# The first expert layer of a two-block transformer kernel: half tiles of 64 rows, two experts at a time in the two column halves of TensorE, in plain fp32

## The chip, the cores and the metric

The kernel runs on one core of a Trainium2 chip. A core has TensorE (matrix products, results in PSUM), VectorE, ScalarE and GpSimd, and SyncE, whose queue issues most of the DMA transfers. The metric is the device time of one execution in microseconds; lower is better.

## The reference, cut to what matters

The whole program is two transformer blocks of two layers each, on 256 tokens of width 1024 (the first block also carries 256 context tokens). The change concerns the mixture of experts of the first layer. It sees 512 tokens, latent and context together:

```python
scores = sigmoid(t @ router_w)
# best group of 4 experts by the sum of its two best scores + bias, then the two best experts in it
combine = one_hot(expert_idx, 16) * normalised_scores          # two experts for each token
def expert(wg, wu, wd, gate_col):                              # wg, wu [1024, 512], wd [512, 1024]
    return gate_col[:, None] * ((silu(t @ wg) * (t @ wu)) @ wd)
out = sum of expert(...) over the 16 experts
```

All arrays are fp32. An expert's three matrices are 2.1 MB each, 6.29 MB together.

## The kernel before, in words

The program is a row of stages with a barrier behind each. The method `experts(layer, tokens)` is the stage of an expert layer: layer 0 with 512 tokens, layer 1 with 256.

The stage begins with the routing. TensorE computes the logits and turns the tokens to rows, which SyncE stores in a DRAM buffer `h_tok`; VectorE ranks the scores and works out, for every token and each of its two experts, a slot: expert e's first 128 tokens have the slots of tile e, and tokens beyond 128 go to overflow tiles 16, 17 and so on. There are `NTILE = 16 + 7 = 23` tiles for 512 tokens, a number fixed at build time, since nothing is known of the routing then. All 23 are computed; an overflow tile that no token needs computes with old weights, because its DMA has a condition (`cond=`, a register loaded from `overflow_in_use_int`) and is skipped.

For each tile GpSimd gathers the token rows from `h_tok` (`tile_rows`), TensorE turns them (`turn_x`, eight transposes) and multiplies: gate (G) and up (U), four pieces each, then down (D), four pieces, of which each is a weight buffer of 128 x 1024 and 512 KB. TensorE runs G and U of tile i, then D of tile i - 1 (`segment(i)`), with `turn_x(i + 1)` ahead of D and `turn_hidden(i)`, four transposes, behind it. The weights lie in the ring areas A (gate), B (up), C and D (down), one expert at a time; a piece is refilled with the next tile's as soon as it is read. The order of the transfers is the order in which SyncE's queue is written: gather results and other stages' panels (`ring.load`, line 83) stand in the same queue.

The products are split in three: ScalarE copies each weight piece to a rounded type (`w_hi`), VectorE forms the remainder (`w_lo`), the same for the turned rows and for the hidden state, and `product` sums hi x hi, hi x lo and lo x hi. ScalarE and VectorE run five pieces ahead (`LEAD`), in six slots.

Results of a tile are copied from PSUM to `tile_out` and stored in `y_slots`. At the end GpSimd waits for all stores, gathers each token's two rows back, and they are mixed, turned and added to the residual.

Of the kernel before, what the change touches and what calls it, by code (L numbers as in the profile page):

```python
# [9 lines left out]
U32 = mybir.dt.uint32  # L10
ALU = mybir.AluOpType
ACT = mybir.ActivationFunctionType
AX = mybir.AxisListType

P = 128
D = 1024
KD = D // P
SEQ = 256
TT = 2 * SEQ
# [12 lines left out]
for _name, _w in VECTORS:  # L32
# [6 lines left out]
CONSTS = [("ident", P), ("ones", P), ("upper", P), ("lower", P), ("up64", P), ("lo64", P),  # L39
          ("xup64", P), ("xlo64", P), ("upper_x", P), ("lower_x", P), ("tie", 16), ("half", 2), ("ropef", 2), ("pair_sum", 2),  # L40
          ("swap_mla", P), ("swap_nsa", P), ("rot_rows", 1), ("causal_add", 2 * P), ("cmp_mask", 32), ("cmp_add", 32)]
ROUTING = [("route_row", P), ("route_base", 16), ("route_over", 16), ("route_before", 256), ("tile_first", 24), ("token_id", 4)]
RCOL, _n = {}, 0
for _name, _w in ROUTING:
    RCOL[_name] = _n
# [1 line left out]
NROUTE = _n  # L47
# [44 lines left out]
@contextmanager  # L92
def stage(nc, names):

    handles = {name: nc.alloc_semaphore(name=f"{name}_{nc.next_id()}") for name in names.split()}
    with nc.Block() as block:  # L96
        yield block, handles
    nc.clear_and_free_semaphores(list(handles.values()))
    nc.all_engine_barrier()


def chain(eng, sem, base=0):

    n = [0]

    def link(ins):
        n[0] += 1
        ins.then_inc(sem, 1)
        eng.wait_ge(sem, base + n[0])
        return n[0]  # L110
    return link


class Program:
# [1025 lines left out]
    def experts(self, layer, tokens):  # L1140
# [4 lines left out]
        nt = tokens // P  # L1145
# [25 lines left out]
        with ExitStack() as ctx:  # L1171
# [54 lines left out]
            with stage(nc, names) as (block, s):  # L1226
# [49 lines left out]
                @block.gpsimd  # L1276
                def _(pool):
                    pool.wait_ge(s["who_done"], 1)
                    pool.wait_ge(s["h_stored"], 16 * nt)
                    for i in range(NTILE):  # L1280
                        if i >= 2:
                            pool.wait_ge(s["x_turned"], i - 1)
                        nc.gpsimd.indirect_dma_start(
                            out=xt[:, i % 2, :], out_offset=None, in_=self.h_tok,
                            in_offset=bass.IndirectOffsetOnAxis(ap=who[:, i:i + 1], axis=0),
                            bounds_check=tokens - 1, oob_is_err=False).then_inc(s[f"xt_in{i % 2}"], 16)
                    pool.wait_ge(s["x_turned"], NTILE)
                    pool.wait_ge(s["stored0"], 16 * ((NTILE + 1) // 2))
                    pool.wait_ge(s["stored1"], 16 * (NTILE // 2))
                    pool.wait_ge(s["rows_done"], 1)  # L1290
                    for t in range(nt):
                        if t >= 2:
                            pool.wait_ge(s["back_turned"], t - 1)
                        for w, (into, sem) in enumerate(((xt, "y0_in"), (y, "y1_in"))):
                            nc.gpsimd.indirect_dma_start(
                                out=into[:, t % 2, :], out_offset=None, in_=self.y_slots,
                                in_offset=bass.IndirectOffsetOnAxis(ap=both_i[:, t, w:w + 1], axis=0),
                                bounds_check=NTILE * P - 1, oob_is_err=False).then_inc(s[f"{sem}{t % 2}"], 16)

# [173 lines left out]
                def _(dve):  # L1473
# [17 lines left out]
                    def hidden_lo(i):  # L1491
                        dve.wait_ge(s["hh_done"], i + 1)
                        V.tensor_tensor(hl[:].rearrange("p k t -> p (k t)"), ps[:, HB, :],
                                        hh[:].rearrange("p k t -> p (k t)").bitcast(F32), ALU.subtract).then_inc(s["hl_done"], 1)
# [92 lines left out]
                    for i in range(NTILE + 1):  # L1587
                        for q, n in enumerate(segment(i)):
                            if n + LEAD < NPIECE:
                                lo(n + LEAD)  # L1590
                            if i < NTILE:
                                if q == 0 and i >= 1:
                                    hidden_lo(i - 1)
                                if q == 7:
                                    hidden(i)
                                if q == (9 if i else 7) and i + 1 < NTILE:
                                    x_lo(i + 1)
                        if i == NTILE - 1:
                            hidden_lo(i)

                    def add(t):
                        dve.wait_ge(s["back_turned"], t + 1)
# [1398 lines left out]
def routing_constants():  # L3001
    c = np.zeros((P, NROUTE), np.float32)
    i, e = np.arange(P), np.arange(16)
    for name, a in (("route_row", i), ("route_base", P * e), ("route_over", P * (15 - e)),
                    ("route_before", (e[None, :] < e[:, None]).reshape(-1)), ("tile_first", P * np.arange(24))):
        c[:, RCOL[name]:RCOL[name] + len(a)] = a
    c[:, RCOL["token_id"]:RCOL["token_id"] + 4] = i[:, None] + P * np.arange(4)[None, :]
    return c
# [86 lines left out]
def everything(p, stop=None):  # L3095
# [4 lines left out]
    if stop == "mix0":  # L3100
        return p.dump()
    p.rms_norm(x, h, KD, TT, lambda k, c: p.scale_mod[:, 1, k, c:c + 1], lambda k, c: p.m(0, 3, k, c))
    p.experts(0, TT)
    if stop == "moe0":
        return p.dump()
    p.rms_norm(x, h, KD, TT, lambda k, c: p.scale_mod[:, 2, k, c:c + 1], lambda k, c: p.m(1, 0, k, c), permuted=True)
# [38 lines left out]
```

## Time and profile before

| | |
|---|---|
| Median of 3 runs | 3425.79 us (3425.68 to 3429.82) |
| The profiled execution | 3423.12 us, span 3421.3 us |
| TensorE busy (records of matmuls) | 2921.3 us, 85% of the span |
| VectorE, ScalarE busy | 2001.9 us (59%), 1513.8 us (44%) |
| DMA over the span | 544.04 MB, mean 159 GB/s |
| Mean granted TensorE clock | 0.914 |

The span runs from the first to the last instruction. A plain fp32 matmul appears in the trace as two records on PE (the matmuls) and two on PEld (the loads of the stationary operand); a transpose and a matmul of the rounded type appear as one each. Matmuls are pipelined, so a record's length is longer than the step to the next one: read the steps between starts.

### The profile page before, as it was taken

The numbers are of one execution on the slowest core, as the hardware profiler recorded it, in microseconds if no ns is written. First come the engines' busy times: TensorE is split into PE (matmuls) and PEld (weight loads), VectorE is DVE, ScalarE is ACT, GpSimd is POOL, SyncE is SP. The second block draws the span as 40 slices with busy tenths as digits, with TensorE's granted clock in tenths as the row PEclk, the third lists the DMA queues.
The fourth block names the chain that finished last, engine by engine and source line by source line (L and its number), as shares of the span: only waits on it lengthen the run. The fifth ranks groups of instructions, "written<-read, shape, count | busy, mean of one in ns | idle before, by whom it ended". The sixth has DMA issues, their size and how long they took to land. (4 is left out here: it accounts for less than half of the span.)

```text
span 3421.3 us, 37051 instructions
## 1 busy us (share of the span) xinstructions
PE 2921.3 (85%) x13538; PEld 2267.2 (66%) x13538; DVE 2001.9 (59%) x2987; ACT 1513.8 (44%) x2268; POOL 266.3 (8%) x223
## 2 busy tenths in 40 slices
PE   4999967777999959986699988986699998877898
PEld 2766556556888836455588867874478787666686
DVE  2597767537999940137589975524555554146554
ACT  2223244335888830023388865421344443025543
POOL 1000024001111000033001100001000000020000
PEclk7999988888999979998799998997699999968999
DMA  5455400127995232110499943531044453400352
GB/s 224 175 209 189 180 1 1 55 79 278 412 412 225 96 116 102 74 50 1 149 383 413 392 158 150 188 135 71 2 184 185 156 192 145 156 23 1 122 192 87
DMA packets 96371, 544.04 MB, mean 159 GB/s; under 512 B 11072, under 2 KB 12480, under 8 KB 72640
## 3 DMA queue, kind: packets, MB, share of 16 engines
q1 hardware_dynamic: 88128, 512.05, 39.2%
q0 software_dynamic: 7776, 28.32, 2.3%
q8 instruction: 109, 1.79, 0.2%
q10 hardware_dynamic: 288, 1.31, 0.1%
q14 instruction: 70, 0.57, 0.1%
HBM read 578.33 MB, written 26.21 MB: 177 GB/s over the span
## 5 line engine op out<-in xcount | busy, mean ns | idle before, releaser
L1135 PE MATMUL ps<-w_hi,x_hi 128*128 128x512 f32 x1440 | 576.4, 400 | 16.6 <-DVE w_lo L2102 8.1
L1137 PE MATMUL ps<-w_hi,x_lo 128*128 128x512 f32 x1440 | 567.2, 394 | 0.0
L1136 PE MATMUL ps<-w_lo,x_hi 128*128 128x512 f32 x1440 | 566.8, 394 | 0.0
L1135 PEld LDWEIGHTS ps<-w_hi,x_hi 128*128 128x128 f32 x1440 | 274.4, 191 | 73.7 <-DVE w_lo L2102 8.7
L1137 PEld LDWEIGHTS ps<-w_hi,x_lo 128*128 128x128 f32 x1440 | 274.2, 190 | 59.3
L1136 PEld LDWEIGHTS ps<-w_lo,x_hi 128*128 128x128 f32 x1440 | 274.9, 191 | 55.1
L1135 PE MATMUL ps<-w_hi,hidden_hi 128*128 128x512 f32 x688 | 271.6, 395 | 9.5 <-DVE hidden_lo L2269 6.0
L1137 PE MATMUL ps<-w_hi,hidden_lo 128*128 128x512 f32 x688 | 268.3, 390 | 0.0
L1136 PE MATMUL ps<-w_lo,hidden_hi 128*128 128x512 f32 x688 | 268.0, 390 | 0.0
L1135 PE MATMUL ps<-x_hi,w_hi 128*128 128x512 f32 (+1 forms) x512 | 214.8, 420 | 55.2 <-DVE x_lo L441 34.7
L1480 DVE TENSOR_TENSOR w_lo<-weights_A,w_hi 128x1024 fp32r<-128x1024 f32 x168 | 204.5, 1220 | 37.5 <-ACT w_hi L1411 34.5
L1411 ACT ACTIVATE w_hi<-weights_A 128x1024 fp32r<-128x1024 f32 x168 | 177.6, 1060 | 69.4 <-PE ps L1137 68.0
L1480 DVE TENSOR_TENSOR w_lo<-weights_B,w_hi 128x1024 fp32r<-128x1024 f32 x168 | 198.1, 1216 | 12.1 <-ACT w_hi L1411 11.8
L1136 PE MATMUL ps<-x_lo,w_hi 128*128 128x512 f32 (+1 forms) x512 | 198.1, 387 | 0.0
L1137 PE MATMUL ps<-x_hi,w_lo 128*128 128x512 f32 (+1 forms) x512 | 197.8, 386 | 0.0
L1411 ACT ACTIVATE w_hi<-weights_B 128x1024 fp32r<-128x1024 f32 x168 | 178.1, 1061 | 41.6 <-PE ps L1137 41.6
L2264 DVE TENSOR_TENSOR w_lo<-weights_A,w_hi 128x1024 fp32r<-128x1024 f32 x96 | 117.5, 1224 | 108.9 <-ACT w_hi L2219 108.9
L2219 ACT ACTIVATE w_hi<-weights_A 128x1024 fp32r<-128x1024 f32 x96 | 101.8, 1061 | 152.8 <-PE ps L1137 104.7
L1135 PEld LDWEIGHTS ps<-x_hi,w_hi 128*128 128x128 f32 x512 | 99.3, 194 | 103.0 <-DVE w_lo L434 36.3
L1135 PEld LDWEIGHTS ps<-w_hi,hidden_hi 128*128 128x128 f32 x688 | 129.3, 188 | 36.1 <-issue 10.8
L1137 PEld LDWEIGHTS ps<-w_hi,hidden_lo 128*128 128x128 f32 x688 | 129.2, 188 | 27.1
L1136 PEld LDWEIGHTS ps<-w_lo,hidden_hi 128*128 128x128 f32 x688 | 129.3, 188 | 25.4
(502 smaller groups left out, 5192.5 us busy)
## 6 DMA issues: line engine op xcount, KB each, us to landing
weights_A<-in_moe_gate SPq DMA_DIRECT2D x160, 512.0 KB
weights_B<-in_moe_up SPq DMA_DIRECT2D x160, 512.0 KB
weights_A<-in_ffn_gu SPq DMA_DIRECT2D x24, 2048.0 KB, 7.5
weights_C<-in_moe_down SPq DMA_DIRECT2D x80, 512.0 KB
weights_D<-in_moe_down SPq DMA_DIRECT2D x80, 512.0 KB
weights_B<-in_ffn_gu SPq DMA_DIRECT2D x20, 2048.0 KB, 7.5
weights_C<-in_ffn_down SPq DMA_DIRECT2D x24, 1024.0 KB, 6.8
y_slots<-tile_out SPq DMA_DIRECT2D x42, 512.0 KB, 7.3
```

The lines of the kernel that those rows point to most:

```text
L1135: nc.tensor.matmul(out, w_hi, x_hi, start=first, stop=False)
L1136: nc.tensor.matmul(out, w_hi, x_lo, start=False, stop=False)
L1137: return nc.tensor.matmul(out, w_lo, x_hi, start=False, stop=last)
L1411: nc.scalar.activation(wh[:, n % SLOTS, :], raw(kind, j), ACT.Copy).then_inc(s["hi_done"], 1)
L1480: V.tensor_tensor(wl[:, n % SLOTS, :], raw(kind, j), wh[:, n % SLOTS, :].bitcast(F32), ALU.subtract).then_inc(s["lo_done"], 1)
L2219: nc.scalar.activation(wh[:, m % SLOTS, :], raw(kind, b, j), ACT.Copy).then_inc(s["hi_done"], 1)
L2264: V.tensor_tensor(wl[:, m % SLOTS, :], raw(kind, b, j), wh[:, m % SLOTS, :].bitcast(F32), ALU.subtract).then_inc(s["lo_done"], 1)
```

## The change

Layer 0 calls a new method `expert_pairs` in place of `experts`; layer 1 keeps the old one. What the new stage does:

- A half tile has 64 rows. Expert e's first 64 tokens go to half tile e, the rest to overflow half tiles, of which there are 15 at build time. Two half tiles 2p and 2p + 1 make pair p, 16 pairs in all (pair 15 has only one).
- The rows of both lie in one tile of 128 rows, gathered and turned together. The first half's products use 64 stationary columns and write partitions 0 to 63 of the PSUM bank, the second half's write partitions 64 to 127, each with its own expert's weights.
- The second half's weights have a buffer of their own, `second_weights`, as large as the ring areas together. It is first filled with expert 1 at the start of the stage.
- The weights are used as they are, in fp32: no `w_hi`, `w_lo`, no split of rows and hidden state, one matmul where there were three.
- The pairs run in the order 0, 1, 15, 2, 3, 14, 4, 5, 13, 6, 7, 12, 11, 10, 9, 8.
- A piece's buffers are refilled for the next position once TensorE has used the piece (`used`), where before it was once VectorE had read it (`lo_done`).

```diff
-    p.experts(0, TT)
+    p.expert_pairs(0, TT)
...
+        R = 64
+        NOV = (2 * tokens - 1) // R
+        NPAIR = 8 + (NOV + 1) // 2
+        PAIRS, late = [], list(range(NPAIR - 1, 7, -1))
+        for p in range(8):
+            PAIRS.append(p)
+            if p % 2:
+                PAIRS += [late.pop(0)] if late else []
+        PAIRS += late
...
+                    for n, (kind, i, j) in enumerate(order):
+                        if i + 1 < NPAIR:
+                            sp.wait_ge(s["used"], n + 1)
+                            if i == 1 and kind == "G" and j == 0:
+                                sp.wait_ge(s["eid_done"], 1)
+                            for h in range(2):
+                                refill(h, kind, i + 1, j)
+                        elif (kind, j) in (("G", 3), ("U", 3), ("D", 1), ("D", 3)):
+                            area = {("G", 3): "A", ("U", 3): "B", ("D", 1): "C", ("D", 3): "D"}[kind, j]
+                            ring.load(sp, area, n + 1, s["used"])
+                        if kind == "U" and j == 3 and i >= 2:
+                            store(i - 2)
+                    store(NPAIR - 2)
+                    store(NPAIR - 1)
...
+                        for c in range(2):
+                            for h in range(2):
+                                half, cols = slice(64 * h, 64 * h + 64), slice(c * 512, (c + 1) * 512)
+                                if kind == "D":
+                                    last = nc.tensor.matmul(ps[half, DB + c, :], hT[:, j, half], raw(h, kind, j)[:, cols],
+                                                            start=(j == 0), stop=(j == 3))
+                                else:
+                                    k = 2 * j + c
+                                    last = nc.tensor.matmul(ps[half, GB if kind == "G" else UB, :], xT[:, i % 2, k, half],
+                                                            raw(h, kind, j)[:, cols], start=(k == 0), stop=(k == KD - 1))
+                        last.then_inc(s["used"], 1)
+
+                    turn_x(0)
+                    for i in range(NPAIR + 1):
+                        for n in segment(i):
+                            if order[n][0] == "D" and order[n][2] == 0 and i + 1 < NPAIR:
+                                turn_x(i + 1)
+                            piece(n)
+                        if i == 0:
+                            turn_x(1)
+                        if i < NPAIR:
+                            turn_hidden(i)
...
+                    def x_copy(i):
+                        act.wait_ge(s["x_turned"], i + 1)
+                        if i >= 2:
+                            act.wait_ge(s["used"], at["U", i - 2, 3] + 1)
+                        for half in range(2):
+                            nc.scalar.activation(xT[:, i % 2, 4 * half:4 * half + 4, :].rearrange("p k t -> p (k t)"),
+                                                 ps[:, XB + half, :], ACT.Copy).then_inc(s["x_done"], 1)
```

TensorE's instructions in the middle of the stage, from the turning of the next rows over the down products, before (in the change the same place follows; `hidden_hi` and `hidden_lo` are the split hidden state, `hidden_turned` the plain one):

```order
1927 L1343 MATMUL ps<-constants,tile_rows 128x128 x8
1928 L1135 MATMUL ps<-w_hi,hidden_hi 128x512
1929 L1136 MATMUL ps<-w_lo,hidden_hi 128x512
1930 L1137 MATMUL ps<-w_hi,hidden_lo 128x512
1931 L1135 MATMUL ps<-w_hi,hidden_hi 128x512
1932 L1136 MATMUL ps<-w_lo,hidden_hi 128x512
1933 L1137 MATMUL ps<-w_hi,hidden_lo 128x512
```

The same place in the change:

```order
1871 L1848 MATMUL ps<-constants,tile_rows 128x128 x8
1872 L1882 MATMUL ps<-weights_C,hidden_turned 64x512
1873 L1882 MATMUL ps<-second_weights,hidden_turned 64x512
1874 L1882 MATMUL ps<-weights_C,hidden_turned 64x512
1875 L1882 MATMUL ps<-second_weights,hidden_turned 64x512
1876 L1882 MATMUL ps<-weights_C,hidden_turned 64x512
```

Three products of 128 rows for one expert have become two of 64 rows, one for each expert, and they alternate between the column halves.

SyncE's queue at the end of the stage, in the change (the last position's down pieces, lines 1764, behind the next stage's panels from `in_hg_in`; an ISA row computes an address):

```order
604 L1764 DMA second_weights<-in_moe_down 128x1024
605 L83 DMA weights_A<-in_hg_in 128x4096
606 L83 DMA weights_B<-in_hg_in 128x4096
607 L1743 DMA y_slots<-tile_out 128x1024
608 L1764 ISA
609 L1764 DMA weights_C<-in_moe_down 128x1024
610 L1764 ISA
611 L1764 DMA second_weights<-in_moe_down 128x1024
```

The panels stood in the same place of the queue before, but the down pieces behind them belonged to an overflow tile whose transfers were skipped.

## Rows read from the trace of the kernel before

**Rows 1.** Busy time of each engine in stretches of the stage, with clock and DMA.
```profile
core 0: us, PE busy (x) PEld busy (x) DVE busy (x) ACT busy (x) POOL busy (x), PEclk, DMA share, GB/s
1000.00:1050.00 50.00, 50.00 (x236) 41.62 (x235) 46.14 (x46) 43.47 (x53) 5.53 (x3) 1.00 1.03 413
1110.00:1160.00 50.00, 50.00 (x241) 41.66 (x240) 46.51 (x45) 42.20 (x51) 4.01 (x2) 1.00 0.15 54
```
**Rows 2.** TensorE's waits from 787 to 1215: waited for, total us, times, longest.
```profile
PE ps L1343 <- DMA tile_rows<-h_tok,token_of_row: 5.9, 1, 5.9
PE ps L1354 <- DVE hidden L1501: 2.1, 1, 2.1
PE ps L1135 <- DVE x_lo L1487: 2.1, 1, 2.1
PE ps L1135 <- ACT tile_out L1438: 1.8, 1, 1.8
```
**Rows 3.** Timeline of TensorE: start us, length us, instructions.
```profile
899.79 0.39 PE L1135 MATMUL ps<-w_hi,x_hi 128*128 128x512 f32 x1
...
909.32 1.03 PE L1343 MATMUL ps<-constants,tile_rows 128*128 128x128 f32 x8
910.11 0.48 PE L1135 MATMUL ps<-w_hi,hidden_hi 128*128 128x512 f32 x1
...
915.65 0.60 PE L1354 MATMUL ps<-constants,hidden 128*128 128x128 f32 x4
...
1110.13 0.60 PE L1354 MATMUL ps<-constants,hidden 128*128 128x128 f32 x4
```
**Rows 4.** DMA from 850 to 1050: totals, and one kind of issue (last: landing).
```profile
DMA packets 22597, 82.40 MB, mean 412 GB/s; under 512 B 2511, under 2 KB 2511, under 8 KB 22584
...
y_slots<-tile_out SPq DMA_DIRECT2D x12, 512.0 KB, 9.6
```
**Rows 5.** The same issue from 1110 to 1180.
```profile
y_slots<-tile_out SPq DMA_DIRECT2D x4, 512.0 KB, 2.6
```
**Rows 6.** Plain fp32 products, 1330 to 1334: ns min/median/max, first and last start.
```profile
L1654 PE MATMUL ps<-weights_A,normed x10: 592/592/593, 1329.8 to 1333.6; 128*128 128x512 f32 x10
```
**Rows 7.** The even mixer, full and half width: timelines of TensorE and its weight loads.
```profile
471.72 0.45 PEld L973 LDWEIGHTS ps<-decay,x_dt 128*64 128x64 f32 x8 [0.67 <-issue]
...
472.88 1.05 PE L941 MATMUL ps<-xbc 128*128 128x128 f32 x8
473.76 1.06 PE L953 MATMUL ps<-constants,log_decay 128*128 128x128 f32 x8
...
507.39 0.45 PE L973 MATMUL ps<-decay,x_dt 128*64 128x128 f32 x4 [0.73 <-issue]
...
508.44 0.48 PE L980 MATMUL ps<-x_w,xb_tokens 128*128 128x256 f32 x1
```
**Rows 8.** Timeline of VectorE in the routing and of TensorE at the first products.
```profile
771.10 0.38 DVE L1542 SCALAR_TENSOR_TENSOR overflow<-position,overflow 128x16 f32<-128x16 f32 x2
...
791.65 0.77 PE L1135 MATMUL ps<-w_hi,x_hi 128*128 128x512 f32 x1 [2.10 <-DVE x_lo L1487]
...
797.34 0.61 PE L1136 MATMUL ps<-w_lo,x_hi 128*128 128x512 f32 x1
797.76 0.42 PE L1137 MATMUL ps<-w_hi,x_lo 128*128 128x512 f32 x1
```
**Rows 9.** Timelines of SyncE, ScalarE and GpSimd at the end of the stage.
```profile
1195.17 0.34 SPq L83 DMA_DIRECT2D weights_C<-in_moe_down  x1
1197.52 0.34 SPq L83 DMA_DIRECT2D weights_D<-in_moe_down  x1
1199.87 7.31 SPq L1241 DMA_DIRECT2D y_slots<-tile_out  x2
...
1205.75 1.09 ACT L1438 ACTIVATE tile_out<-ps 128x512 f32<-128x512 f32 x2 [5.90 <-PE ps L1137]
...
1210.28 0.99 POOL L1295 DMA_INDIRECT tile_rows<-y_slots,two_rows_int  x1 [67.31 <-DMA y_slots<-tile_out]
```

More of the change, by code:

```diff
@@ L41 @@
           ("swap_mla", P), ("swap_nsa", P), ("rot_rows", 1), ("causal_add", 2 * P), ("cmp_mask", 32), ("cmp_add", 32)]
-ROUTING = [("route_row", P), ("route_base", 16), ("route_over", 16), ("route_before", 256), ("tile_first", 24), ("token_id", 4)]
+ROUTING = [("route_row", P), ("route_base", 16), ("route_over", 16), ("half_base", 16), ("half_over", 16), ("route_before", 256), ("tile_first", 24), ("token_id", 4)]
 RCOL, _n = {}, 0
@@ L1295, in _ @@
                             nc.gpsimd.indirect_dma_start(
-                                out=into[:, t % 2, :], out_offset=None, in_=self.y_slots,
+                                out=into[:, t % 2, :], out_offset=None, in_=self.y_slots[0:NTILE * P, :],
                                 in_offset=bass.IndirectOffsetOnAxis(ap=both_i[:, t, w:w + 1], axis=0),
@@ L1599, in _, with add @@
                             hidden_lo(i)
+                    def add(t):
+                        dve.wait_ge(s["back_turned"], t + 1)
+                        for k in range(KD):
+                            rows = X[:, k, t * P:(t + 1) * P]
+                            V.scalar_tensor_tensor(out=rows, in0=ps[:, 2 * (t % 2) + k // 4, (k % 4) * P:(k % 4 + 1) * P],
+                                                   scalar=self.m(layer, 5, k, t // 2), in1=rows,
+                                                   op0=ALU.mult, op1=ALU.add).then_inc(s["added"], 1)
@@ new lines, in _ @@
+                    for t in range(nt):
+                        dve.wait_ge(s["weighed"], t + 1)
+                        dve.wait_ge(s[f"y1_in{t % 2}"], 16 * (t // 2 + 1))
+                        V.scalar_tensor_tensor(out=xt[:, t % 2, :], in0=y[:, t % 2, :], scalar=share[:, t, 1:2], in1=xt[:, t % 2, :],
+                                               op0=ALU.mult, op1=ALU.add).then_inc(s["mixed"], 1)
+                        if t >= 1:
+                            add(t - 1)
+                    add(nt - 1)
@@ L3003, in routing_constants @@
     i, e = np.arange(P), np.arange(16)
-    for name, a in (("route_row", i), ("route_base", P * e), ("route_over", P * (15 - e)),
+    for name, a in (("route_row", i), ("route_base", P * e), ("route_over", P * (15 - e)), ("half_base", 64 * e), ("half_over", 64 * (15 - e)),
                     ("route_before", (e[None, :] < e[:, None]).reshape(-1)), ("tile_first", P * np.arange(24))):
```

344 lines of the change are left out of this document (added).

## The prediction

> **What bounds the kernel now.** The change touches one stage, the first expert layer, so I read that stage and its two ends. First the page, for the span in the table above, then the engines' busy time in stretches of the stage [rows 1]: TensorE is busy 50.00 of 50 us both while weights arrive at 413 GB/s and later, when 54 GB/s move, with about 240 records in each stretch. Its list of waits over the whole stage has four rows, each a single wait of at most 5.9 us [rows 2]. So TensorE's own work bounds the stage, 23 tiles of it. The timeline gives the size of a tile [rows 3]: from one group of hidden transposes (L1354 at 915.65) to that of eleven tiles later (1110.13) it is 194.48 / 11 = 17.68 us. Inside it 42 split matmuls take from 899.79 to 909.32, a step of 0.227 us; the eight transposes of the rows take 0.79 until the next product. The four of the hidden state take the rest: 17.68 less 72 steps of 0.227 and 0.79 leaves 0.55, the slower first steps behind transposes in it.
>
> The same stretches show a second resource next to its limit. DMA stands at a share of 1.03 with 413 GB/s [rows 1]. Over 200 us that is 22597 packets and 82.40 MB, 100.6 packets of 4 KB per us [rows 4]. A tile wants 12 x 128 packets of weights, 128 of gathered rows and 128 of stored rows, 1792 in 17.68 us, which is 101.4 per us. A store lands in 9.6 us there and in 2.6 us once weights are no longer fetched [rows 4, 5]. I read this as a full queue that delivers just what TensorE asks for.
>
> **What the change asks of DMA.** With the drawn inputs the 512 tokens give the 16 experts 71 56 70 77 79 68 84 71 72 45 54 69 48 55 49 56 rows. None passes 128, so before only 16 tiles fetch weights, and the last seven fetch nothing (their lines are skipped by the condition). Nine pass 64, so after the change nine half tiles of overflow, numbers 16 to 24, are in use and fetch an expert's 6.29 MB a second time. The positions of the new loop fetch for 2 2 0 2 2 0 2 2 0 2 2 1 2 2 2 2 half tiles: pairs 15, 14 and 13 hold none that is in use, pair 12 one, and pairs 11, 10, 9, 8 stand last. Half tiles 0 and 1 are there before the loop starts.
>
> **TensorE's new price.** A plain fp32 product of 512 columns is two records. Ten records of one full-width chain have their first and last start 3.8 us apart [rows 6], nine steps of 0.427. The question is whether the two column halves run at once. The even mixer has matmuls of 64 output columns that alternate between the halves of a bank, in plain fp32, with 128 moving columns [rows 7]. The three groups of four left out there are like the one shown; sixteen such records fill 507.39 to 508.44, 1.05 us. Eight full-width ones of the same length fill 472.88 to 473.76, 0.88 us, 0.11 each. Taking 0.11 off for the change of tiling at the end, the halves give 0.94 / 16 = 0.059 us each. They do overlap, nearly wholly, with 0.006 per record left over. For 512 columns I take two products, one per half, as 2 x (0.427 + 0.012) = 0.878 us. A pair has 24 of these, 21.1 us; the transposes 1.7 together, 1.34 as now and some 0.1 for each of four changes between half and full width. A position is then 22.8 us of TensorE, and 16 of them 365 us against 23 x 17.68 = 407. The splitting on ScalarE and VectorE goes away and gives nothing by itself: TensorE waited for `x_lo` once, at the start [rows 2].
>
> The page "TensorEngine Tiling (Array Packing)" of the Trainium skill (Key Properties) says that a change of tiling mode drains the engine. The trace shows about 0.11 us for it, less than 0.5 us in a position. The page "TensorE: Matmul & The Clock Gate" (Part 3) says that weight loads overlap running matmuls only where the row group differs. Both halves use the same rows here, so by it no load would be hidden. By that rule a position would cost what the second rival below gives; the half-width steps above speak against it.
>
> **Where the time goes instead.** A pair with two fetching halves needs 24 x 128 + 256 = 3328 packets, 33.1 us at 100.6 per us. That is more than 22.8. Groups of two such pairs and an idle one take 68.7 us of DMA and 68.4 us of TensorE, so up to position 8 TensorE sets the pace. A piece's buffer is refilled only once the piece was used, so nothing is fetched further ahead than one position. From the first use at position 8 (8 x 22.8 + 1.8 = 184 us after the first product) the queue is never empty. It has to move the weights of positions 9, 10, 11 and 12 to 15 (19968 packets) and about six gathers and stores (1536), 213.8 us. The next stage's first two panels, 2 MB each, are issued once the gate and up pieces of the last position are used, ahead of that position's four down pieces: 4.2 MB at 412 GB/s, 10.2 us. The last piece adds 1.2 for landing and 1.8 for its products. Sum: 184 + 213.8 + 10.2 + 3.0 = 411 us. I stepped all 192 pieces by the same rules (in order on both engines) and came to 410.6, with TensorE's stalls at positions 12 to 15.
>
> Before, the same stretch is 791.65 to 1205.75, 414.1 us [rows 8, 9].
>
> **The ends.** At the start the clock is at its lower level, 1.2 GHz, 0.42 us a step against 0.227, until about 797.8 [rows 8]; that costs about 2.8 us in either kernel and is not in the 411. The first hidden state is waited for 2.1 us [rows 2], again in both. The first product comes 0.4 us earlier: the residual copy on VectorE goes (part of the 2.1 us waited for it), and six comparisons of 0.19 us stand in the routing in place of two [rows 8]. The twelve first loads of the second buffer, 15 us of traffic at 412 GB/s, are issued at the stage's start and lie beside the routing, with nothing else in the queue then but 2 MB of stores; I cost them at nothing, and at 5 us if a store waits behind them. TensorE's end is 791.2 + 411 + 2.8 + 2.1 = 1207.1, against 1205.75: +1.4.
>
> Then the last store. Before, the next stage's C and D panels went out at 1195.17 and 1197.52, well before the two stores (1199.87 to 1207.2), and the first gather of results starts at 1210.28, 4.5 us behind the last product [rows 9]. After, D's panel is issued with the last product used, 1 MB ahead of both stores in one queue: 2.5 + 1.3 + 1.3 for three transfers and about 2 to land, 7.1 us. That is +2.6. Gathers, mixing and everything later are as before. Sum: +1.4 + 2.6 = **+4.0 us**. The profiled execution took 3423.1 (span 3421.3) and the median is 3425.8, so I forecast **3430 us**.
>
> About 0.2%, 6.9 us, is what a measurement of this kernel can tell from no change.
>
> **Bounds of the unknown prices.** Two products in the halves: from 0.853 (nothing left over; the stepping gives 410, since the queue takes up the rest) to two full chains one behind the other, 1.73. The queue: from 100 to 109 packets per us (the last would be 447 GB/s, above the 413 of any stretch of the stage [rows 1]). With 109 the stepping gives 392, with 100 it gives 413; I take 100.6, the rate delivered.
>
> **Rivals.**
>
> - *The queue was not full* (faster). Then the 412 GB/s [rows 4] are only TensorE's demand, and the four last positions cost less. For it: delivery is within 1% of demand. Against it: a landing of 9.6 us against 2.6, and the share of 1.03. At 109 packets per us: 411 to 392, 19 us less, 3411 us. With no limit at all 16 x 22.8 + 3 = 368, 3387 us. Chance 0.14.
> - *Weight loads show, or the clock falls, so TensorE is slower than 0.878* (slower). Eight loads of 64 columns take 0.45 us, 0.056 each [rows 7]. Shown in full, 96 of them add 5.4 us to a position, 1.10 for two products; the stepping gives 456 instead of 411, so 3475 us. It decides early, since up to position 8 every position passes its excess on: 0.90 for two products gives 414 and is the edge of the 0.2%, 0.93 gives 419 (3438 us), 1.0 gives 433. The clock: TensorE would work 21 of 33 us in the last positions, with gaps below 1 us; at half clock a piece takes 3.5 us against 2.5 of its transfer. Chance of either, with 4 to 50 us lost, 0.20.
> - *The halves don't overlap at 512 columns* (slower). Two products then take 1.73, a position 43.2 us, TensorE never waits for the queue, and the stepping gives 692: 281 us more, 3711 us. The half-width steps speak against it [rows 7]. Chance 0.04.
> - *My small terms add to more than 7 us* (slower): the queue loses a little to the mixture of two experts' rows, register loads ahead of the conditional transfers, or ends later than reckoned; 3433 to 3445. Chance 0.17.
> - *The forecast*, within 0.2%: 0.45.
>
> The last two are one mechanism; its own range is 3417 to 3445. The whole range reaches to the first rival's 3411 and to most of the second: 3412 to 3465. Faster: 0.14. Same: 0.45. Slower: 0.20 + 0.04 + 0.17 = 0.41.
>
> **What the profile after would show.** Right: in the stage, GB/s near 412 from position 9 on, TensorE busy throughout up to there and waiting for weight DMAs in the last 130 us, some 33 us from one position to the next; products in the halves paired 0.43 apart; positions of about 22.8 us at the start; ScalarE and VectorE nearly idle. Wrong: positions of 28 us or more with no DMA wait (loads or clock), of 43 us (no overlap), DMA beyond 420 GB/s (a queue that was not full), or a number of fetching half tiles other than nine, which moves the end by 15 us for each.

## The result and the profile after

The changed kernel takes 3427.68 us (median of 20 runs, 3421.61 to 3430.74), the kernel before 3421.1 us over its 20 runs of the same comparison. The ratio is 1.0016, 95% interval 1.0009 to 1.0023: 5.5 us longer (3 to 8), which is clear of zero and within the 0.2% that was called no change; the two medians lie 6.6 us apart. The forecast was 3430 us: +4.0 us, put on the median of 3425.8 that the first three runs of the kernel before had.

The profiled execution took 3425.3 us, span 3423.4. First the busy times of the page of the changed kernel: us, share of the span, instructions.

```profile
PE 2874.8 (84%) x13334; PEld 2050.7 (60%) x13334; DVE 1636.9 (48%) x2639; ACT 1218.4 (36%) x1950; POOL 240.4 (7%) x216
```

Then its stretches of the stage, the same view as [rows 1], with two short ones at the end:

```profile
core 0: us, PE busy (x) PEld busy (x) DVE busy (x) ACT busy (x) POOL busy (x), PEclk, DMA share, GB/s
850.00:900.00 50.00, 50.00 (x241) 17.56 (x238) 1.38 (x2) 6.52 (x12) 1.98 (x2) 1.00 1.03 418
1000.00:1050.00 50.00, 49.82 (x240) 17.43 (x238) 1.38 (x2) 6.63 (x13) 2.73 (x3) 1.00 1.03 418
1060.00:1180.00 120.00, 92.08 (x402) 29.66 (x400) 2.77 (x4) 11.95 (x22) 0.99 (x1) 0.99 1.03 421
1110.00:1160.00 50.00, 39.26 (x170) 12.62 (x172) 0.69 (x1) 5.43 (x10) 0.00 (x0) 1.00 1.03 419
1180.00:1190.00 10.00, 3.27 (x8) 1.14 (x10) 0.00 (x0) 0.00 (x0) 0.00 (x0) 0.50 1.00 412
```

VectorE went from 46 to 1.4 us of 50 and ScalarE from 43 to 6.6, which by itself bought nothing (e4_plain_full_tiles, below, leaves the splitting out without pairing the halves, and is slower). What matters is the change of bound inside the stage. Up to 1050 TensorE is busy all the time, as in [rows 1]. From then on it is busy 39 us of 50, while DMA stays at a share of 1.03 with 419 GB/s, where before it had dropped to 54 GB/s. TensorE's waits from 787 to 1215 have new names against [rows 2] (waited for, total us, times, longest; the list goes on with two rows of 3.4 us for which it names no releaser, "issue"):

```profile
PE ps L1882 <- DMA second_weights<-in_moe_down: 16.2, 11, 10.9
PE ps L1886 <- DMA second_weights<-in_moe_up: 7.4, 12, 1.3
PE ps L1886 <- DMA second_weights<-in_moe_gate: 7.0, 12, 1.2
```

The timeline of TensorE shows the halves side by side, the answer to [rows 3] and [rows 6], then three pieces of a late position, then the end of the stage (start us, length us):

```profile
792.32 0.59 PE L1886 MATMUL ps<-weights_A,x_turned 128*64 128x512 f32 x1
792.34 0.59 PE L1886 MATMUL ps<-second_weights,x_turned 128*64 128x512 f32 x1
792.75 0.59 PE L1886 MATMUL ps<-weights_A,x_turned 128*64 128x512 f32 x1
...
1146.46 0.61 PE L1886 MATMUL ps<-weights_A,x_turned 128*64 128x512 f32 x1 [0.59 <-DMA second_weights<-in_moe_gate]
1148.96 0.61 PE L1886 MATMUL ps<-weights_A,x_turned 128*64 128x512 f32 x1 [0.57 <-DMA second_weights<-in_moe_gate]
1151.44 0.61 PE L1886 MATMUL ps<-weights_A,x_turned 128*64 128x512 f32 x1 [0.54 <-DMA second_weights<-in_moe_gate]
...
1186.73 1.08 PE L1882 MATMUL ps<-weights_C,hidden_turned 128*64 128x512 f32 x1 [10.93 <-DMA second_weights<-in_moe_down]
1186.74 1.12 PE L1882 MATMUL ps<-second_weights,hidden_turned 128*64 128x512 f32 x1
1187.61 1.06 PE L1882 MATMUL ps<-weights_C,hidden_turned 128*64 128x512 f32 x1
...
1192.89 0.59 PE L1882 MATMUL ps<-weights_D,hidden_turned 128*64 128x512 f32 x1
```

Two records, one of each expert, start every 0.43 us. Late in the stage a piece (both experts' 512 KB) comes every 2.49 us, which is TensorE's pace there. Before the last down pieces it stands still for 10.93 us, and the granted clock is 0.50, the 1.2 GHz level, in 1180 to 1190: behind the wait the step is 0.86 instead of 0.43, and the eight pairs of records of area C take 6.2 us, to 1192.89, where they take 3.4 at full clock: 2.7 us more.

SyncE and GpSimd at the end, in answer to [rows 9]:

```profile
1159.24 1.03 SPq L83 DMA_DIRECT2D weights_A<-in_hg_in  x1
1164.05 0.34 SPq L83 DMA_DIRECT2D weights_B<-in_hg_in  x1
...
1176.09 0.33 SPq L1764 DMA_DIRECT2D second_weights<-in_moe_down  x1
1193.11 0.34 SPq L83 DMA_DIRECT2D weights_C<-in_moe_down  x1
1196.54 0.34 SPq L83 DMA_DIRECT2D weights_D<-in_moe_down  x1
1196.92 1.06 SPq L1743 DMA_DIRECT2D y_slots<-tile_out  x2
...
1208.13 0.99 POOL L1800 DMA_INDIRECT tile_rows<-y_slots,two_rows_int  x1 [132.50 <-DMA y_slots<-tile_out]
```

The next stage's panels A and B go out at 1159 and 1164, ahead of the last four down pieces of each of the two experts (1168 to 1176). D's goes out at 1196.54, with the last product used, ahead of both stores: the first of them, of a position long done, waits in SyncE's order for that load to be issued.

The stage in four parts, for every kernel profiled in this study, in us. They are: from the load of the router's weights, its first issue, to the first product; from there to the end of the last product; from there to the first gather of results; from there to the next stage's first load, of `lb_rows` (all three taken from the starts in the timelines and in the views of one line). The names of the experiments are explained below. The time is the ratio to the kernel before, of each one's own comparison.

| kernel | to first product | products | to gather | to next stage | sum | ratio (95%) |
|---|---|---|---|---|---|---|
| before | 45.2 | 414.1 | 4.5 | 50.9 | 514.7 | 1 |
| changed | 45.5 | 411.6 | 11.6 | 53.4 | 522.1 | 1.0016 (1.0009 to 1.0023) |
| e2_no_second_fetch | 45.4 | 364.0 | 11.7 | 52.3 | 473.4 | 0.9887 (0.9871 to 0.9904) |
| e3b_one_half | 45.5 | 692.1 | 11.3 | 52.1 | 801.0 | a single run: 3708.5 us |
| e4_plain_full_tiles | 44.4 | 507.9 | 10.0 | 51.3 | 613.6 | 1.029 (1.0273 to 1.0307) |
| e1_panels_later | 45.4 | 400.2 | 16.1 | 52.5 | 514.2 | 1.0003 (0.9994 to 1.0012) |
| e8_cd_last | 45.5 | 411.5 | 6.7 | 51.6 | 515.3 | 1.0 (0.9991 to 1.0009) |
| e6_panels_last | 45.5 | 401.1 | 7.0 | 52.3 | 505.9 | 0.997 (0.9958 to 0.9982) |
| e5_queue_ahead | 45.4 | 403.0 | 11.4 | 52.4 | 512.2 | 0.999 (0.9981 to 0.9999) |
| e7_both | 45.7 | 393.0 | 6.2 | 51.6 | 496.5 | 0.9952 (0.9938 to 0.9965) |
| e9_halves_apart | 45.5 | 411.2 | 11.7 | 52.7 | 521.1 | 1.0024 (1.0013 to 1.0035) |
| e10_before_panels_last | 45.1 | 414.4 | 6.8 | 51.8 | 518.0 | 0.9997 (0.9988 to 1.0006) |

Between the two kernels of the change the products are 2.5 us shorter and the rest 9.9 us longer. The load of the router's weights starts at 746.4 in the profiled execution of before and at 739.4 in that of after, but the code up to there is the same; e10_before_panels_last, which is the kernel before up to that point, has 741.8. The other profiles lie between 737.6 and 741.8, so that of the kernel before stands apart. These 7 us are spread from one execution to the next, and only the parts inside the stage are compared.

### The profile page after: what moved, and what is told of

The parts are those of the page before. It is cut to its first block and busy times, and to the rows that moved or that the text cites. A ratio compares the mean times of both kernels' runs of the same rounds, so it can differ in the third digit from the quotient of the medians.

```text
span 3423.4 us, 35997 instructions
## 1 busy us (share of the span) xinstructions
PE 2874.8 (84%) x13334; PEld 2050.7 (60%) x13334; DVE 1636.9 (48%) x2639; ACT 1218.4 (36%) x1950; POOL 240.4 (7%) x216
## 5 line engine op out<-in xcount | busy, mean ns | idle before, releaser
L1135 PE MATMUL ps<-w_hi,x_hi 128*128 128x512 f32 x1072 | 429.1, 400 | 14.2 <-DVE w_lo L2559 8.1
L1137 PE MATMUL ps<-w_hi,x_lo 128*128 128x512 f32 x1072 | 422.6, 394 | 0.0
L1136 PE MATMUL ps<-w_lo,x_hi 128*128 128x512 f32 x1072 | 422.1, 394 | 0.0
L1886 PE MATMUL ps<-second_weights,x_turned 128*64 128x512 f32 x512 | 231.4, 601 | 0.0
L2721 DVE TENSOR_TENSOR w_lo<-weights_A,w_hi 128x1024 fp32r<-128x1024 f32 x96 | 117.6, 1225 | 108.5 <-ACT w_hi L2676 108.5
L2676 ACT ACTIVATE w_hi<-weights_A 128x1024 fp32r<-128x1024 f32 x96 | 101.9, 1061 | 152.7 <-PE ps L1137 104.6
L718 DVE SCALAR_TENSOR_TENSOR normed<-u,vectors,normed 128x512 f32<-128x512 f32 x210 | 146.2, 759 | 0.8
L1886 PE MATMUL ps<-weights_A,x_turned 128*64 128x512 f32 x256 | 117.7, 606 | 10.5 <-DMA second_weights<-in_moe_gate 7.0
L1886 PE MATMUL ps<-weights_B,x_turned 128*64 128x512 f32 x256 | 114.8, 593 | 9.4 <-DMA second_weights<-in_moe_up 7.4
L1882 PE MATMUL ps<-second_weights,hidden_turned 128*64 128x512 f32 x256 | 118.5, 609 | 0.0
```

What stands on the lines that cost most here:

```text
L718: nc.vector.scalar_tensor_tensor(out=out, in0=windows(c, j), scalar=self.v("cf_w", KD * j + c), in1=out, op0=ALU.mult, op1=ALU.add).then_i ...
L1135: nc.tensor.matmul(out, w_hi, x_hi, start=first, stop=False)
L1136: nc.tensor.matmul(out, w_hi, x_lo, start=False, stop=False)
L1137: return nc.tensor.matmul(out, w_lo, x_hi, start=False, stop=last)
L1882: last = nc.tensor.matmul(ps[half, DB + c, :], hT[:, j, half], raw(h, kind, j)[:, cols], start=(j == 0), stop=(j == 3))
L1886: last = nc.tensor.matmul(ps[half, GB if kind == "G" else UB, :], xT[:, i % 2, k, half], raw(h, kind, j)[:, cols], start=(k == 0), stop=(k ...
```

## Experiments

**Is it the second fetch?** The theory after the result: the queue's bytes bound the stage from the ninth position on, and the panels and stores at its end stand in the same queue. The first rival is TensorE itself, with products that got dearer.

```diff
-  link(V.tensor_scalar(busy[:], eid[:], 16.0, None, ALU.is_lt))
+  link(V.tensor_scalar(busy[:], eid[:], 0.0, None, ALU.is_lt))
```

> The comparison that finds overflow tiles in use never holds here, so the nine overflow half tiles in use fetch no weights and are worked with whatever their buffers hold (tokens beyond an expert's 64 get wrong values); the products, their number and all else stay. Theory 1 (the queue's bytes bound the first-layer expert stage from its ninth position on, 1.5 MB x 4 x 9 of them fetched twice): the stage's loop falls from 411.6 us to TensorE's own 16 positions x 22.56 = 361 and a few us for both ends, so the kernel takes 44 to 48 us less than the changed one, about 3380 (0.988 of the kernel before). Theory 2 (the half-width products and their weight loads bound it, the queue is only busy beside them): nothing changes, 1.0016 of the kernel before. Theory 3 (the half before is slowed by granted clock alone): nothing changes.

Measured: 0.9887, about 44 us less than the changed kernel; products 364.0 us instead of 411.6. Over the products 108.13 MB move instead of 164.86: 56.7 MB less, nine times an expert's 6.29. The waits for weights are gone but one (TensorE in e2_no_second_fetch, 787 to 1165):

```profile
PE ps L1886 <- ACT x_turned L1918: 2.2, 2, 1.3
PE ps L1882 <- ACT hidden_turned L1925: 1.3, 1, 1.3
PE ps L1882 <- DMA second_weights<-in_moe_down: 0.8, 1, 0.8
```

So the nine second fetches cost 44 to 48 us, and TensorE's own 16 positions are 364 us with both ends. Weight loads, dearer products or the granted clock as the bound (theories 2 and 3) are refuted.

**Do the halves have to be two halves?**

```diff
+  low = slice(0, 64)
-  matmul(ps[half, ...], ..., start=(k == 0), stop=(k == KD - 1))
+  matmul(ps[low, ...], ..., start=(k == 0 and h == 0), stop=(k == KD - 1 and h == 1))
   (the down products in the same way)
```

> Both experts' products are written to partitions 0 to 63, so that both use the same half of the array's columns, and are summed up in one group (the output is wrong); number of products, weight loads and transfers stay. Theory 1 (a pair of products in the two halves takes 0.86 us because the two run at the same time): a pair now takes two products after each other, 2 x 0.86 = 1.72 us, a position 24 x 1.72 = 41.3 us and 3 us of turns, 16 of them 709 in place of 411.6: the kernel takes about 3725 us. Theory 2 (a 64-column product is by itself half as long as one of 128 columns, the place in the array doesn't matter): no change, 3427.

Measured: 3708.5 us in a single run, products 692.1 us; its list of waits names no weights. The timeline of TensorE in e3b_one_half shows the two experts' records one behind the other, a record each 0.43 us:

```profile
830.82 0.59 PE L1887 MATMUL ps<-weights_A,x_turned 128*64 128x512 f32 x1
831.25 1.02 PE L1887 MATMUL ps<-second_weights,x_turned 128*64 128x512 f32 x2
832.11 1.02 PE L1887 MATMUL ps<-weights_B,x_turned 128*64 128x512 f32 x2
```

A 64-column product is not shorter than one of 128; only the place in the other half lets two go on together. (The edit moves the array's columns and the partitions of PSUM together; which of the two keeps the records apart is not told by it.) The expectation of 3725 was some 17 us too high, since it took 3 us of turns a position on top of 41.3: 692.1 / 16 is 43.3, turns and ends in it.

**What is the pairing worth, without the splitting?** Tiles of 128 rows, one expert at a time, plain fp32:

```diff
-  R = 64
+  R = 128
-  NPAIR = 8 + (NOV + 1) // 2
+  NPAIR = 16 + NOV
   (one expert a position, half = slice(0, P), no second set of loads)
```

> The plain fp32 products without the halves: tiles of 128 rows as before the change, one expert at a time (16 + 7 positions), weights used as they come with no split, everything else as in the changed kernel; nothing is left out. Theory 1 (the plain fp32 product costs 0.86 us per 512 columns and the two halves together cost the same, so that the pairing is what pays for it): a position takes 24 x 0.86 us and 1.5 of turns, 22 us, against 17.68 with the split, so 23 x (22 - 17.68) = +100 us: 1.029 of the kernel before, about 3520. Theory 2 (leaving out the split's work on VectorE and ScalarE, or the fewer turns, is what keeps the time level, and the pairing adds little): within 10 us of the kernel before.

Measured: 1.029, products 507.9 us, 22.08 a position, with no wait for weights in the list. Plain fp32 costs as much for one expert of 128 rows as for two of 64, 22.1 against 22.6 a position. The step from before to after thus has three parts: leaving the split costs 94 us (414.1 to 507.9), the pairing, 16 positions in place of 23, gives back 144 (507.9 to 364.0, e2_no_second_fetch), and the second fetches take 48 of these.

**Which panels cost what?** First A and B alone, behind the last down pieces:

```diff
-  elif (kind, j) in (("G", 3), ("U", 3), ("D", 1), ("D", 3)):
-      ring.load(sp, area, n + 1, s["used"])
+      if n == at["D", NPAIR - 2, 3]:   # after the refill
+          ring.load(sp, "A", n + 1, s["used"])
+          ring.load(sp, "B", n + 1, s["used"])
+  elif (kind, j) in (("D", 1), ("D", 3)):
+      ring.load(sp, "CD"[j // 2], n + 1, s["used"])
```

> One part moved: the next stage's first two 1.5 MB panels (areas A and B) are issued behind the last position's twelve refills of the down pieces, not ahead of them. Theory 1 (the 10.9 us that TensorE waits at 1186.7 for the last down pieces, and the drop of the granted clock to its lower level behind it, come from those two panels standing ahead in a full queue): the wait goes, and the stage ends 10 to 13 us earlier; the last stores may wait a few us more behind the panels; 0.996 to 0.998 of the kernel before (changed kernel 1.0016). Theory 2 (the queue is fair to all transfers in flight, so that the order of issue does not matter, only the bytes before the end): less than 3 us gained, 1.0008 to 1.0016. Theory 3 (the next stage then waits for its panels): the gain is given back after the stage, no change in sum.

Measured: 1.0003. The mechanism is right and the size is off: the wait goes (the longest for down weights is 1.3 us), the products are 11.4 us shorter, but the stores now stand behind A and B too, and the way to the gather grows from 11.6 to 16.1. (Each panel is 2 MB, not the 1.5 that the expectation says.) Of the 11.4 us, 4.5 go back there, and the timed comparison keeps about 4.4 (1.0016 - 1.0003, of 3421), with an uncertainty nearly as large. Theory 3 did not come about: the way to the next stage is 52.5 us, not longer than the changed kernel's. Theory 2, that only the bytes count, has the measured time within its reach but not the trace, where the wait is gone.

Then C and D alone, issued after the gathers:

```diff
+  for t in range(2):
+      sp.wait_ge(s[f"y1_in{t}"], 16 * (nt // 2))
+  ring.load(sp, "C", len(order), s["used"])
+  ring.load(sp, "D", len(order), s["used"])
```

> The other half of the panels' move by itself: areas C and D (1 MB each) are issued after the gathers that end the stage, A and B stay ahead of the last down pieces as in the changed kernel. Theory 1 (two separate costs: the wait of 10.9 us belongs to A and B, and some 4 to 5 of the 11.6 us between last product and first gather belong to C and D, since with all four moved that stretch was 7.0): the 10.9 us wait stays, the tail falls to about 7, and the kernel takes 4 to 5 us less than the changed one, 1.0002 of the kernel before. Theory 2 (the tail is late through A and B too, which still land then): the tail stays at 11, 1.0016.

Measured: 1.0, way to the gather 6.7 us, and the long wait is there as before (TensorE in e8_cd_last):

```profile
1188.71 1.09 PE L1885 MATMUL ps<-weights_C,hidden_turned 128*64 128x512 f32 x1 [10.94 <-DMA second_weights<-in_moe_down]
```

Then all four after the gathers (the same wait, with `for area in "ABCD"`):

> All four panels of the next stage (A, B, C, D, 5 MB) are issued after the gathers that end this stage, so that neither the last down pieces nor the last two stores have them ahead in the queue. Theory 1 (the changed kernel loses about 10.9 us with its clock drop before the last down pieces, and about 7 of its 11.6 us between last product and first gather, to these panels): 17 to 20 us less than the changed kernel if the panels still land before the next stage wants them (they are first used some 50 us later): 0.996 of the kernel before. Theory 2 (only the last down pieces matter, the stores are late for another reason, for example their own 8 KB rows written by 64 partitions): as with A and B alone, 10 to 13 us. Theory 3 (the panels become late for the next stage, which waits at its start): no gain or a loss.

Measured: 0.997, some 16 us less than the changed kernel: 10.5 in the products and 4.6 on the way to the gather, where theory 1 had 17 to 20 with 7 in the second. (The four panels are 6 MB together, not the 5 of the expectation.) The panels are issued 30 us ahead of the next stage's first load, and the list of TensorE's waits from 1240 to 1330 names no panel. SyncE in e6_panels_last:

```profile
1186.82 0.33 SPq L1743 DMA_DIRECT2D y_slots<-tile_out  x1
...
1213.43 0.34 SPq L83 DMA_DIRECT2D weights_A<-in_hg_in  x1
...
1214.76 0.84 SPq L83 DMA_DIRECT2D weights_D<-in_moe_down  x1
...
1244.99 0.33 SPq L2089 DMA_DIRECT2D lb_rows<-in_lb_rows  x1
```

So theory 1 holds for both costs, the A and B wait with its slow clock and the C and D panels ahead of the stores.

**Is the idle queue early in the stage worth something?** In the changed kernel 259 GB/s move from 805 to 830 (first row), in e5_queue_ahead 419 (second row):

```profile
805.00:830.00 25.00, 25.00 (x122) 9.57 (x120) 0.69 (x1) 3.26 (x6) 0.99 (x1) 1.00 0.68 259
...
805.00:830.00 25.00, 25.00 (x124) 9.43 (x121) 0.69 (x1) 3.26 (x6) 0.99 (x1) 1.00 1.03 419
```

```diff
-  PAIRS.append(p); if p % 2: PAIRS += [late.pop(0)] ...
+  PAIRS = [0, 1, 2, 15, 3, 4, 14, 5, 6, 13, 7, 12, 11, 10, 9, 8]
```

> Only the order of the pairs: overflow pairs later by one position or two, so that the fetches per position are 2 2 2 (1 or 0) 2 2 0 ... and the queue, which is idle for some 13 us between the second and third position of the changed kernel, is kept fed. Theory 1 (the queue's bytes bound the stage, so time that it is idle early is lost at the end): 8 to 10 us less than the changed kernel, 0.999 of the kernel before. Theory 2 (the end is set by the last position's waits alone, or by TensorE): no change, 1.0016.

Measured: 0.999, products 8.6 us shorter. As expected, bytes that pass early need not pass at the end. With both:

> The later overflow pairs and the four panels after the gathers together. Theory 1 (both act on the same resource, the bytes that must pass before the last product, so the gains add): 25 to 29 us less than the changed kernel, 0.993 to 0.994 of the kernel before, about 3400. Theory 2 (once the panels are out of the way, TensorE's 361 us plus start or the last position bounds, and the order brings nothing more): as with the panels alone, 17 to 20 us less.

Measured: 0.9952, 3402.12 us median: the fastest version here, 16 us below the kernel before and about 22 below the changed one. The stage's sum is 25.6 us shorter than the changed kernel's in the profile, as theory 1 had it; by the timed ratios it is 22 us, a little short of the 25 to 29 expected. The single gains add up to 25 (9 and 16), which their intervals don't tell from 22. By time alone the 17 to 20 of theory 2 would not be excluded either; the trace decides, where the products are 8.1 us shorter than with the panels alone (401.1 to 393.0).

**Do the panels help the kernel before as well?** The same four loads after the gathers, in the first layer of the kernel before:

> The kernel before the change, with the one thing that helped the changed one: in the first-layer expert stage all four panels are issued after the gathers. Theory 1 (TensorE bounds that kernel to the last product, so no transfer ahead of it is missed, and its tail is 4.5 us already): 0 to 2 us gained, 0.9995 to 1.000. Theory 2 (the panels are a burden in whatever kernel, the gain of 16 us is not owed to the change): 10 us or more, 0.997.

Measured: 0.9997, no difference. Its products are 414.4 us, the kernel before has 414.1. At the end of that kernel's stage the queue is not full (54 GB/s from 1110 to 1160, [rows 1]), so there is nothing to free; what e6_panels_last gains is a cost that the change had brought in.

**Must the two halves alternate in the program?**

```diff
-  for c in range(2):
-      for h in range(2):
+  for h in range(2):
+      for c in range(2):
```

> Only the order of the four products of a piece: both of the first expert, then both of the second, where the changed kernel alternates between the halves. Theory 1 (the halves work independently and products start in order: of first-first-second-second the middle two run together, and the last one runs with the first of the next piece): a piece in an unbroken run still takes two slots of 0.86 us, and only after each break (a turn, a wait for a piece) one slot of 0.86 more; the early, TensorE-bound positions take 22.6 + 3 breaks x 0.86 = 25, and the later ones, bound by the queue, stay; the queue is idle longer early, so the kernel takes 5 to 25 us more, 1.003 to 1.009 of the kernel before. Theory 2 (only a directly following pair within its piece overlaps): three slots for a piece, 12 x 0.86 = 10.3 us more for each of 16 positions, of which the queue-bound ones hide some 9: about 70 to 165 us more. Theory 3 (the order doesn't matter at all): 1.0016.

Measured: 1.0024, its interval overlaps with that of the changed kernel; products 411.2 against 411.6, and four positions, from one group of row transposes to the fourth after it, take 90.45 us (818.31 to 908.76) against 90.23. Theory 2 falls. Neither does a break cost the slot that theory 1 charged: a position takes 22.61 us there and not 25 (by the interval alone the lower end of theory 1 would still fit). Theory 3 is what the trace shows. The timeline shows why: the second expert's first record starts beside the first expert's, though two products of the first stand ahead of it in the program (TensorE in e9_halves_apart, behind the transposes):

```profile
819.33 0.64 PE L1882 MATMUL ps<-weights_C,hidden_turned 128*64 128x512 f32 x1
819.35 0.64 PE L1882 MATMUL ps<-second_weights,hidden_turned 128*64 128x512 f32 x1
819.81 0.59 PE L1882 MATMUL ps<-weights_C,hidden_turned 128*64 128x512 f32 x1
819.83 0.59 PE L1882 MATMUL ps<-second_weights,hidden_turned 128*64 128x512 f32 x1
```

## Why the prediction was right, and where its terms were off

The forecast of no change held, and so did its mechanism: TensorE's gain, 50 us of products (414.1 to 364.0), is eaten by nine second fetches (364.0 to 411.6 in e2_no_second_fetch against the changed kernel) once the queue never runs empty. That the sum of +4.0 lies so near the +5.5 measured is in part luck: its terms were off in both directions, by up to 4.5 us.

- **"A position is then 22.8 us", "2 x (0.427 + 0.012) = 0.878".** Measured 22.56 (90.23 / 4) and 0.86 for two products: nothing is left over for the change of half. What the prediction took for a change between half and full width, 0.11, no row shows: it is the step of one full-width record. In [rows 7] the groups left out start at 507.63, 507.85 and 508.07, a step of 0.055 a record, and the change then takes 0.15. In the changed kernel it takes 0.13 (step of 0.56 at the first row, where 0.43 is that of a pair) and 0.14 back:

```profile
816.80 0.59 PE L1886 MATMUL ps<-weights_B,x_turned 128*64 128x512 f32 x1
817.36 1.09 PE L1848 MATMUL ps<-constants,tile_rows 128*128 128x128 f32 x8
818.38 0.64 PE L1882 MATMUL ps<-weights_C,hidden_turned 128*64 128x512 f32 x1
```

  Over the eight positions before the queue takes over that is 2 us too many. The page "TensorE: Matmul & The Clock Gate" of the Trainium skill (Part 3), by which no load would be hidden behind a matmul of the same rows, is not borne out: the loads are busy 17.4 of 50 us in 1000 to 1050 while the pairs keep their step of 0.43.
- **"A full queue that delivers just what TensorE asks for", 100.6 packets per us.** The queue was full, but the rate is not that of the changed kernel. Where TensorE waits for each piece, a piece of 1.049 MB takes 2.49 us: 421 GB/s, 2% more. On the 224 us of queue time (213.8 + 10.2) that makes 4 to 5 us less. It is not a spare rate that TensorE failed to ask for: the DMA share is 1.03 in both kernels, and from 850 to 900 418 GB/s move although TensorE waits for nothing there. In the records of the packets one of 4 KB takes 162 ns in mean before (850 to 1050) and 159 after. Why they are slower before, where stores and gathers are a larger part and VectorE and ScalarE are busy, was not tested. The first rival had the right sign here, but not its cause and not the size: 421 GB/s are 103 packets of 4 KB per us, and 109 were not reached.
- **The panels A and B ahead of the last down pieces, 10.2 us.** Right: a wait of 10.93, and e1_panels_later removes 11.4 us of products. What the term lacks is the granted clock behind such a wait, 0.50, 2.7 us.
- **The products in all.** The prediction had 411 + 2.8 + 2.1 = 415.9; measured 411.6. The positions (-2), the queue (-4 to -5), the clock behind the long wait (+2.7) and the wait for the first hidden state, of which 0.9 of 2.1 us is left (a wait for `x_turned` at 803.48), give that within about 1 us.
- **The start, "0.4 us earlier".** Measured 0.2 later, 45.48 against 45.24. The first loads of the second buffer, costed at nothing, are not free: e4_plain_full_tiles, which does not have them, needs 44.4. With them the stores of the token rows, which the prediction had priced at 5 us if they waited, land 4 us later (25.9 us after the stage's first load, where it is 21.7 before and 21.5 in e4), but the first gather is issued only 1.1 us later than in e4 (37.7 against 36.6), since it waits for VectorE's routing. So they cost about 1 us; they were not tested alone.
- **The last store, 7.1 us after the last product.** Measured 11.6. The order was right, D's panel ahead of both stores. The mistake is the price of the three transfers: 412 GB/s were taken for them, and they get less (the changed kernel; the columns are those of the stretches above; every engine stands still by then):

```profile
1198.00:1200.00 2.00, 0.00 (x0) 0.00 (x0) 0.00 (x0) 0.00 (x0) 0.00 (x0) 0.75 0.72 250
1200.00:1202.00 2.00, 0.00 (x0) 0.00 (x0) 0.00 (x0) 0.00 (x0) 0.00 (x0) 0.50 0.90 244
1202.00:1204.00 2.00, 0.00 (x0) 0.00 (x0) 0.00 (x0) 0.00 (x0) 0.00 (x0) 0.50 0.97 385
1204.00:1206.00 2.00, 0.00 (x0) 0.00 (x0) 0.00 (x0) 0.00 (x0) 0.00 (x0) 0.50 0.37 145
```

  The last store lands 9.6 us after its issue. With no panel near (e7, e8, e6) it still lands only 4.2 to 5.0 us after it, for a reason given in the last section. Even then the way to the gather is 7.0 us (e6_panels_last). The panels C and D are worth 4.6 to 4.9 of it (e6 and e8).
- **"Gathers, mixing and everything later are as before."** 53.4 us against 50.9 in this pair of profiles. The ten other profiles have 51.3 to 52.7, and e10_before_panels_last, whose code in this part is that of the kernel before but for the panels, which it issues there, 51.8. So perhaps 1 of the 2.5 us is what two executions differ by; the rest was not tested and stays open.

Start +0.2, products -2.5, store +7.1 and mixing +2.5 make +7.3 in this pair of profiles; the forecast had -0.4, +1.8, +2.6 and 0.

The rivals: weight loads that show were refuted by e2 (22.8 us a position with its ends, 364.0 / 16), halves that don't overlap by the pairs in the trace and by e3b, which has the time they would have cost; a queue with room fell on the share of 1.03 and on its size.

## What to carry to other kernels

When a change moves the bound to a queue, everything that rides in that queue becomes part of the critical path: the next stage's prefetch, harmless before (e10: 0.9997), cost 16 us after (e6), and queue time left idle early cost 9 (e5). So a change that trades one engine's work for bytes has to be made together with the order of the transfers; done so, it gained 0.5% here in place of losing 0.16%. A rate that is read from a full queue holds for the traffic and the neighbours that it had there: the same share of 1.03 was 412 GB/s before and 417 to 421 after. Give such a term a range of a few per cent, and look for a stretch in which somebody waits for each piece.

## What the runs showed of the hardware that was not expected

- Products in the two column halves need not stand beside each other in the program. In e9_halves_apart the order was first, first, second, second, and the records still show a pair every 0.43 us. How far apart they may stand was not tried.
- The landing of a store can hang on a transfer that stands in no queue of the program. In e10_before_panels_last the last two stores of the stage both have the queue to themselves. The first is issued at 1195.45 and lands after 2.6 us, the second at 1202.44 and lands after 4.8. The DMA views of the two (1194 to 1200, then 1202 to 1208):

```profile
GB/s 0 0 0 0 0 0 0 0 0 0 0 0 0 0 0 382 410 410 382 382 437 410 437 246 0 0 0 0 0 0 0 0 0 0 0 0 0 0 0 0
y_slots<-tile_out SPq DMA_DIRECT2D x1, 512.0 KB, 2.6
...
GB/s 0 0 0 0 0 0 0 0 246 464 382 410 410 382 382 328 382 0 0 0 27 0 0 27 0 27 27 27 27 27 27 0 0 0 0 0 0 0 0 0
q8 instruction: 1, 0.02, 1.8%
y_slots<-tile_out SPq DMA_DIRECT2D x1, 512.0 KB, 4.8
```

  All but a few packets move as fast in the second, and 15 of the store's 16 closing packets are through 2.3 us after its issue, as in the first. In between one packet of 16 KB of the queue for instructions starts at 1203.44 and takes 1.7 us, and the store's remaining packets come one behind the other after it, the last at 4.3 us. The last stores of e6, e7 and e8 hold the same single packet, and land after 4.2 to 5.0 us; in the kernel before it passed at 1203.05, ahead of the last store, which was issued at 1206.86 and landed after 2.6. That is why the way from the last product to the gather is 6.8 us in e10 against 4.5. It is read from five traces; no run moved that packet.
- After 10.93 us without work TensorE's granted clock was at its 1.2 GHz level (0.50 in 1180 to 1190), and the pair step 0.86 for about 5 us; where the gaps were 0.5 to 1.8 us each (e6_panels_last, and the positions from 1060 on) the mean clock stayed at 0.99 to 1.00.
